# First mixer of a two-mixer decoder step: values and decayed keys turned by VectorE and a DRAM scratch instead of by TensorE

## The reference

```python
def hgrn_layer(x, s0, norm_g, w_in, g_norm, w_o, lb):
    proj = rms_norm(x, norm_g) @ w_in
    q, fz, i, gate = jnp.split(proj, [hk, 2 * hk, 2 * hk + A_WIDTH], axis=-1)
    q = silu(q)
    logf = jnp.logaddexp(jnp.log(lb), jnp.log1p(-lb) + log_sigmoid(fz))
    k = (1.0 - lb) * sigmoid(-fz)
    v = i
    o, s_t = gated_recurrence(q, k, v, logf, s0, chunk)
    o = rms_norm(o, g_norm) * silu(gate)
    return x + o @ w_o, s_t
...
def step(s, inp):                      # one chunk of one head
    cum = jnp.cumsum(gc, axis=2)
    o_inter = einsum('bhtk,bhkv->bhtv', qc * exp(cum), s)
    decay = exp(where(causal, cum[:, :, :, None, :] - cum[:, :, None, :, :], -inf))
    att = einsum('bhtk,bhsk,bhtsk->bhts', qc, kc, decay)
    o = o_inter + einsum('bhts,bhsv->bhtv', att, vc)
    s_new = exp(last)[..., None] * s + einsum('bhsk,bhsv->bhkv', kc * exp(last - cum), vc)
```

## Time and profile before

| | |
|---|---|
| Median of 3 runs | 1513.93 us (1513.2 to 1513.94) |
| The profiled execution's own time | 1510.86 us |
| Its span, first to last instruction | 1509.1 us |
| TensorE busy | 1476.7 us, 98% |
| VectorE busy | 987.5 us, 65% |
| ScalarE busy | 677.9 us, 45% |
| GpSimd busy | 418.0 us, 28% |
| Mixer A's heads | from 51.58 us to some 592.8 us of the span |
| One inner head (head 3) | 68.15 us |

### The profile page before, as it was taken

How to read it: one execution, slowest core, us unless ns; L and a number is a source line. 1 busy time by engine, 2 the same in 40 slices (tenths; PEclk the granted TensorE clock), 3 DMA queues, 4 the chain that set the end, 5 groups by cost and what they waited for, 6 DMA issues and landing times.

```text
span 1509.1 us, 23379 instructions
## 1 busy us (share of the span) xinstructions
PE 1476.7 (98%) x8437; PEld 1089.3 (72%) x8437; DVE 987.5 (65%) x1987; ACT 677.9 (45%) x1380; POOL 418.0 (28%) x335
## 2 busy tenths in 40 slices
PE   6999999999999999999999999999999999998998
PEld 6788888888888885445777777777777777763443
DVE  5878696878778694126467676868777676757321
ACT  4444555444444453212265555645555555545100
POOL 5012322121212201012051535354352625422200
PEclk9999999999999999999999999999999999999999
DMA  9683939476583933423236859696877869598731
GB/s 275 186 234 103 292 95 267 137 208 184 164 228 113 291 140 111 126 64 129 62 112 191 271 180 310 191 278 201 270 247 229 274 214 308 179 341 329 242 131 58
DMA packets 290505, 300.53 MB, mean 199 GB/s; under 512 B 25863, under 2 KB 247295, under 8 KB 290391
## 3 DMA queue, kind: packets, MB, share of 16 engines
q1 hardware_dynamic: 279254, 262.44, 57.1%
q0 software_dynamic: 11136, 36.59, 6.7%
HBM read 243.57 MB, written 122.53 MB: 243 GB/s over the span
## 4 chain that ended last, share of the span: by engine, by line
PE 86%; DVE 5%; ACT 4%; DMA 2%; issue 2%; SPq 0%; POOL 0%; DVEq 0%; POOLq 0%
PE psum L2145 44%; PE psum L2169 7%; PE psum L2659 7%; PE psum L2457 5%; PE psum L2483 4%; PE psum L2222 3%; PE psum L2108 2%; PE psum L2417 2%; PE psum L2515 2%; ACT psum L1281 1%; PE psum L2308 1%; PE psum L2292 1%; PE psum L2233 1%; ACT psum L1290 1%; PE psum L2310 1%
## 5 line engine op out<-in xcount | busy, mean ns | idle before, releaser
L2145 PE MATMUL psum<-arena 128*128 128x252 f32 (+1 forms) x3472 | 811.9, 385 | 2.3 <-DVE arena L1458 2.2
L2145 PEld LDWEIGHTS psum<-arena 128*128 128x128 f32 x3472 | 640.7, 190 | 124.8 <-issue 23.1
L956 POOL TENSOR_TENSOR arena<-arena 128x1024 f32<-128x1024 f32 x64 | 156.8, 2450 | 377.8 <-DMA arena<-k_pages 373.1
L1458 DVE TENSOR_TENSOR arena<-arena,psum 128x252 f32<-128x252 f32 (+1 forms) x310 | 128.9, 416 | 160.0 <-PE psum L2145 155.1
L2659 PE MATMUL psum<-arena 128*128 128x512 f32 x256 | 113.9, 597 | 1.6 <-DVE arena L1872 1.6
L2169 PE MATMUL psum<-arena 128*128 128x512 f32 x256 | 113.0, 594 | 0.1
L1031 ACT COPY arena<-psum 128x252 f32<-128x252 f32 (+1 forms) x124 | 46.2, 372 | 138.3 <-PE psum L2145 138.2
L2659 PEld LDWEIGHTS psum<-arena 128*128 128x128 f32 x256 | 47.1, 190 | 59.4 <-issue 57.0
L2169 PEld LDWEIGHTS psum<-arena 128*128 128x128 f32 x256 | 47.5, 190 | 57.4 <-issue 56.5
L1094 ACT ACTIVATE arena<-arena 128x1024 f32<-128x1024 f32 x48 | 50.7, 1056 | 84.6 <-DVE arena L1504 84.2
L1281 ACT ACTIVATE psum<-psum,arena 128x640 f32<-128x640 f32 (+3 forms) x64 | 58.9, 921 | 61.0 <-DVE arena L1805 61.0
(11 more groups left out here) (272 smaller groups left out, 2083.2 us busy)
## 6 DMA issues: line engine op xcount, KB each, us to landing
k_pages<-in_cache_k SPq DMA_DIRECT2D x64, 512.0 KB, 6.5
v_pages<-in_cache_v SPq DMA_DIRECT2D x64, 512.0 KB, 7.1
arena<-k_pages SPq DMA_DIRECT2D x64, 512.0 KB, 5.4
arena<-v_pages SPq DMA_DIRECT2D x64, 512.0 KB, 6.8
arena<-in_w_in_a SPq DMA_DIRECT2D x32, 512.0 KB, 6.8
arena<-in_x_prompt SPq DMA_DIRECT2D x16, 512.0 KB, 7.5
arena<-in_w_kv SPq DMA_DIRECT2D x16, 512.0 KB, 6.8
arena<-in_w_in_b SPq DMA_DIRECT2D x16, 512.0 KB, 8.0
```

The costliest lines, as they stand in the source:

```text
L956: pool.tensor_tensor(k_ring[:, m % 2], k_ring[:, m % 2], q_all[:, m % S:m % S + 1, :].broadcast_to([P, PAGES, P]), ALU.mult).then_inc(kq_m ...
L1458: dve.tensor_tensor(out, more, bank[n % 2][:, 0:size(u)], ALU.add).then_inc(of.by_dve, 1)
L2145: ins = pe.matmul(bank[n % 2][:, 0:size(u)], w[:, k, :], x[:, k, :], start=(k == 0 and r in (0, 1, 3, 4)), stop=(k == HK - 1), skip_group_ ...
```

## The change

In mixer A the sixteen transposes of a head on TensorE (L2258 and L2276) and ScalarE's four copies (L1121, L1146) are gone. VectorE turns V and the decayed keys in blocks of 32 x 32 from SBUF to SBUF (`turn_tokens`); SP writes each to a DRAM tensor `token_rows` with four DMAs and reads it back with one (`tokens_out`, `tokens_in`), which puts the blocks in place. After the way back the 128 columns of a chunk stand in four groups of 32 that are apart from one another, so where V or the keys are the stationary operand, each matmul becomes four of 32 columns: 32 instead of 8 for the state updates, and 32 instead of 8 for V by att. The updates move behind `fq(9)` (in the last head behind `fq(8)`), and the state part of the outputs into a loop of its own. The exponential for `k_dec` and `k_dec` itself move ahead, and `k_dec` lies in `t1` now. The copy of `o_row` moves ahead of the gate's step. SP's sorting of pages is cut in two halves of 8 DMAs a head. On GpSimd the F and Q sums of head h + 2 are made at the end of `head(h)`, from unit 11 of the running `fq` on, and the store of `s_smp` goes ahead of the V and G sums.

```diff
@@ VectorE
+                def turn_tokens(n, out, src):
+                    dve.transpose(out.rearrange("p (r t l) -> p t r l", r=4, l=32),
+                                  src.rearrange("p (t r l) -> p t r l", r=4, l=32)).then_inc(blocks_turned, 2)
...
                 factors(2)
                 fq(1)
+                dve.wait_ge(*units.taken(vg_unit(h, 9)))
+                dve.wait_ge(*units.taken(vg_unit(h, 12)))
+                turn_tokens(0, v_blocks, raw_v[:, 0:T])
                 merge(4)
+                a("exp_kd")
+                dve.tensor_tensor(k_dec, k_h[:, 0:T], t1[:, 0:T], ALU.mult).then_inc(vecs.sem, 1)
+                dve.wait_ge(vecs.sem, vecs.at("k_dec", h))
+                turn_tokens(1, k_blocks, k_dec)
                 a("s_kept")
...
                 merge(2)
                 fq(4)
-                a("exp_kd")
-                dve.tensor_tensor(k_dec, k_h[:, 0:T], t1[:, 0:T], ALU.mult).then_inc(vecs.sem, 1)
                 merge(1)
                 fq(5)
+                dve.wait_ge(smp_done.sem, smp_done.at("o_row", h))
+                dve.tensor_copy(o_row, bank[6][:, 0:2 * P]).then_inc(vecs.sem, 1)
                 a("ln_g")
...
-                dve.wait_ge(smp_done.sem, smp_done.at("o_row", h))
-                dve.tensor_copy(o_row, bank[6][:, 0:2 * P]).then_inc(vecs.sem, 1)
...
+                fq(8)
                 chunk_states(0)
-                fq(8)
                 chunk_states(1)
@@ SP
-            for h in range(AH - 1):
-                sp.wait_ge(units.done, vg_unit(h, 14))
...
-                sort_pages(sp, h + 1)
...
+            for s, half in ((0, 0), (0, 1), (1, 0)):
+                sort_pages(sp, s, half)
+            def tokens_out(h, n, blocks):
+                sp.wait_ge(blocks_turned, 2 * token_set(h, n))
+                if h:
+                    sp.wait_ge(pt_moved, MOVES * token_set(h - 1, n))
+                dst = token_rows[n].rearrange("(r l) (g n) -> g l r n", r=4, g=4)
+                for g in range(4):
+                    src = blocks[32 * g:32 * g + 32].rearrange("p (r n) -> p r n", r=4)
+                    sp.dma_start(dst[g], src).then_inc(rows_stored, 16)
+            def tokens_in(h, n, blocks):
+                sp.wait_ge(rows_stored, STORES * token_set(h, TOKEN_SETS - 1 if h == AH - 1 else n))
+                sp.dma_start(blocks, token_rows[n]).then_inc(pt_moved, 16)
+            for h in range(AH):
...
+                if h < AH - 1:
+                    tokens_out(h, 0, v_blocks)
+                sp.wait_ge(units.done, vg_unit(h, 14))
+                if h + 2 < AH:
+                    load_w(sp, h // 2 + 1, h % 2)
+                elif h + 2 == AH:
+                    sp.dma_start(w_o[:, 0:AH // 2], w_o_rows[:, 0:AH // 2]).then_inc(w_o_loaded, 16)
+                else:
...
+                    tokens_out(h, 0, v_blocks)
+                if h < AH - 1:
+                    tokens_in(h, 0, v_blocks)
+                    tokens_out(h, 1, k_blocks)
+                else:
+                    tokens_out(h, 1, k_blocks)
+                    tokens_in(h, 0, v_blocks)
+                tokens_in(h, 1, k_blocks)
+                if h < AH - 1:
+                    sort_pages(sp, h + 1, 1)
...
+                    if h + 2 < AH:
+                        sort_pages(sp, h + 2, 0)
@@ TensorE
-                    for t in range(4 * j, 4 * j + 4):
-                        ins = pe.transpose(bank[4 + j][:, t % 4 * P:(t % 4 + 1) * P], raw_v[:, cols(t)], ident)
...
-                    for t in range(4 * j, 4 * j + 4):
-                        ins = pe.transpose(bank[4 + j][:, t % 4 * P:(t % 4 + 1) * P], k_dec[:, cols(t)], ident)
...
-                fq(8, 9, 10)
+                fq(8)
+                if h + 1 < AH:
+                    fq(9)
+                pe.wait_ge(pt_moved, MOVES * token_set(h, 1))
+                for j in range(2):
+                    pe.wait_ge(uu_taken_v, 4 * h + 5 + j)
+                    for c in range(4 * j, 4 * j + 4):
+                        for g in range(4):
+                            ins = pe.matmul(bank[4 + j][32 * g:32 * g + 32, c % 4 * P:(c % 4 + 1) * P], k_dec_tok[:, block_of(c), g],
+                                            v_tok[:, block_of(c)], start=True, stop=True, skip_group_check=True)
+                    ins.then_inc(uu_done.sem, 1)
+                if h + 1 == AH:
+                    fq(9)
+                fq(10)
...
+                    for g in range(4):
+                        pe.matmul(bank[6 + t // 4][32 * g:32 * g + 32, t % 4 * P:(t % 4 + 1) * P], v_tok[:, t, g], att[:, cols(t)],
+                                  start=(t % 4 == 0), stop=(order[t] == 0), skip_group_check=True)
@@ GpSimd, head(h)
-                if h + 1 < AH:
-                    if h:
-                        pool.wait_ge(units.done, fq_unit(h, 14))
-                    w_sums(h + 1, F, Q, sums_fq, fq_sums)
+                if h == 0:
+                    w_sums(1, F, Q, sums_fq, fq_sums)
                 if 0 < h < AH - 1:
                     o_store(h - 1)
+                pool.wait_ge(uu_taken_v, 4 * h + 6)
+                pool.dma_start(state_out[h], s_smp).then_inc(state_stored, 16)
                 if h + 1 < AH:
                     pool.wait_ge(units.done, vg_unit(h, 14))
                     w_sums(h + 1, V, G, sums_vg, vg_sums)
-                pool.wait_ge(uu_taken_v, 4 * h + 6)
-                pool.dma_start(state_out[h], s_smp).then_inc(state_stored, 16)
                 pool.wait_ge(uu_taken_v, 4 * h + 8)
                 pool.dma_start(prompt_out[h], s_all[:, NC - 1, :]).then_inc(prompt_stored, 16)
+                if h + 2 < AH:
+                    pool.wait_ge(units.done, fq_unit(h + 1, 11))
+                    w_sums(h + 2, F, Q, sums_fq, fq_sums, last_free=(units.done, fq_unit(h + 1, 13)))
```

More of the change, by code:

```diff
@@ L487, in build, with token_set @@
         HEAD = (slice(0, DH), slice(DH, P))
+        def token_set(h, n):
+            return TOKEN_SETS * h + n + 1
         def row_banks(i):
@@ L545, in page_id, with sort_pages @@
             return sp.value_load(at, min_val=0, max_val=n_pool - 1)
-        def sort_pages(sp, s):
-            for j in range(PAGES):
+        def sort_pages(sp, s, half):
+            for j in range(HALF * half, HALF * half + HALF):
                 page = page_id(sp, s * PAGES + j)
@@ L585, in _ @@
-            sp.wait_ge(o_stored, 16 * (AH - 2))
-            sp.wait_ge(vecs.sem, vecs.at("q", AH - 1))
-            for h in range(EARLY):
-                sp.dma_start(o_heads[h], o_dram[h]).then_inc(early_loaded, 16)
-            sp.wait_ge(units.done, vg_unit(AH - 1, 14))
-            for h in range(EARLY, AH - 2):
-                sp.dma_start(o_heads[h], o_dram[h]).then_inc(o_loaded, 16)
-            sp.dma_start(w_o[:, AH // 2:AH], w_o_rows[:, AH // 2:AH]).then_inc(w_o_loaded, 16)
-            LF_STEP = -(-S * PAGES // (TT - 1))
+            for s, half in ((0, 0), (0, 1), (1, 0)):
+                sort_pages(sp, s, half)
@@ L816, in _, with block_sums @@
             me = Steps(pool, w_steps)
-            def block_sums(one, two, out, done):
+            def block_sums(one, two, out, done, last_free=None):
                 me.did(pool.tensor_tensor(out[:, 0], two[:, 0:HK], two[:, HK:KT], ALU.add))
@@ L1116, in head @@
                 level(8)
+                for t in range(NC):
+                    end = t * P if t >= NC // 2 else t * P + C - 1
+                    ins = act.activation(t1[:, cols(t)], cum[:, cols(t)], ACT.Exp, bias=cum[:, end:end + 1], scale=-1.0)
+                ins.then_inc(acts.sem, 1)
                 level(4)
                 level(2)
-                for j in range(2):
-                    act.wait_ge(uu_done.sem, uu_done.at(f"v_turn{j}", h))
-                    act.copy(v_tok[:, 4 * j:4 * j + 4, :], bank[4 + j][:, :]).then_inc(uu_taken_a, 1)
                 fq(0)
@@ L1133, in head @@
                 fq(2)
-                for t in range(NC):
-                    end = t * P if t >= NC // 2 else t * P + C - 1
-                    ins = act.activation(t1[:, cols(t)], cum[:, cols(t)], ACT.Exp, bias=cum[:, end:end + 1], scale=-1.0)
-                ins.then_inc(acts.sem, 1)
                 act.wait_ge(*units.taken(vg_unit(h, 13)))
@@ L1143, in head @@
                 act.activation(sg_h, sg_h, ACT.Ln, bias=1.0).then_inc(acts.sem, 1)
-                for j in range(2):
-                    act.wait_ge(uu_done.sem, uu_done.at(f"turn{j}", h))
-                    act.copy(k_dec_tok[:, 4 * j:4 * j + 4, :], bank[4 + j][:, :]).then_inc(uu_taken_a, 1)
                 v("o_smp")
@@ L2271, in head @@
                 fq(5)
-                v("k_dec")
-                for j in range(2):
-                    pe.wait_ge(uu_taken_v, 4 * h + 5 + j)
-                    for t in range(4 * j, 4 * j + 4):
-                        ins = pe.transpose(bank[4 + j][:, t % 4 * P:(t % 4 + 1) * P], k_dec[:, cols(t)], ident)
-                    ins.then_inc(uu_done.sem, 1)
```

(14 more changed lines are left out.)

70 lines of the change are left out of this document (36 added, 34 removed).

## The result

The changed kernel takes **1538.64 us** (median of four runs, 1537.44 to 1541.54); the kernel before, run beside it, 1513.58 us. The ratio is 1.0165 [1.0153, 1.0177]: slower, by 25.1 us. The prediction was slower by 9.2 us, 1523 with a range up to 1532; the sign is right, the size is not, and the time lies above the range.

A forecast was written before the change was run, and what follows sets the result against it. TensorE, busy for 98% of the span, was taken as the bound. Six heads +6.9, head 6 -0.45, head 7 +2.8 gave +9.2 us on the 1513.93 median: 1523, range 1506 to 1532.

The forecast's parts named there:

- What leaves and what comes on TensorE: TensorE, each head: transposes leave (-1.76 us), strips come (+0.56), net -1.20 us without a new wait.
- The strips' part: State updates and V by att in 32-column strips on TensorE: +0.28 us a block, +0.56 a head.
- Rival D: TensorE's strips stop overlapping in runs of 64: 7.1 us a block, +85 us, 1599; chance 0.01.
- VectorE's turns: Two block transposes a head, 0.6 to 1.25 us each; V turned by 292.4, K by 295.6, hidden from TensorE.
- K's wait: TensorE before state updates, for K's DRAM round trip: 2.5 us a head taken, 2.8 worked out.
- rival C: K's blocks return from DRAM before TensorE asks, transfers at 405 GB/s: -8.5 us, 1505.4; chance 0.24.
- The sums made sooner: GpSimd's F and Q sums a head sooner: TensorE waits for none of them, priced at zero.
- rival E: VectorE late for fact1 or merges, transposes slowed beside GpSimd: 1 to 2 us a head, 1522; chance 0.03.
- Head 7: Last head: V by att starts +2.5 us later behind K's and V's reloads, +0.28 for strips: +2.8 us.
- A: The wait before the state updates decides, as summed: 1523, own range 1517 to 1532; chance 0.58.
- B: The wait just eats the saving: 0.6 to 1.6 us in each of seven heads, about 1514; chance 0.14.
- F: GpSimd's sums made sooner do nothing: 0 us, held true in all cases, no separate chance.

The follow-up runs named there:

- late_w: Changed kernel with the next weights' load (or first half of w_o) issued behind K's reload instead of ahead of V's: 1506.27 us, ratio 0.9957.
- strips: Kernel before with only the state updates and V by att in 32-column strips, transposes kept: 1518.57 us, ratio 1.003.
- w_first: Changed kernel with SP issuing the next weights (w_o in head 6) ahead of V's stores: 1518.64 us, ratio 1.0035.
- upd_late: Changed kernel with state updates two units later, behind fq(11), and VectorE's gate step ahead of chunk_states; DMAs untouched: 1508.72 us, ratio 0.9969.
- sums_later: Changed kernel with GpSimd's F and Q sums waiting for unit 12 instead of 11, nothing else: 1533.94 us, ratio 1.0133.
- sums_only: Kernel before with only GpSimd's F and Q sums made a head sooner: 1512.89 us, ratio 0.9996.
- late_w_split: late_w with the waits for q_dec and chunk_states moved behind the last units' V-by-att strips: 1505.91 us, ratio 0.9953.
- sums_back: Changed kernel with GpSimd's F and Q sums of head h + 1 back at their old place, at the start of head h: 1535.26 us, ratio 1.0144.
- best2: late_w_split with GpSimd's F and Q sums starting one unit later: 1504.45 us, ratio 0.9935.
- w_first_sums: w_first with GpSimd's F and Q sums back at their old place: 1514.33 us, ratio 1.0002.

## Why the prediction was right and wrong

**What leaves and what comes on TensorE: right.** -1.20 us a head was forecast without a new wait; `late_w`, whose inner heads have no wait, gives 67.04 against 68.15, -1.11. The strips' part was 0.56, `strips` measured 0.65 a head: the updates 1.88 to 1.89 us as said with the way in, the output block a little dearer. Rival D had no case.

**VectorE's turns: right, at the dear end.** The block transpose from SBUF takes 1.24 us; V is turned at 302.97, which is 292.4 on the old scale (10.53 us later in the span), the number given. K is turned at 306.09, 295.6 on the old scale, again the number given.

**K's wait: the mechanism right, the size 2.5 against some 3.0 in heads 1 to 5.** On the old scale TensorE reaches the updates at 309.7 (forecast 309.6) and K's tokens are there at 312.9; the working had found 312.4, a wait of 2.8, and I then took 2.5 of it. K out was issued at 300.8, not 299, because V's way back took 1.81 us to issue behind the weights (0.34 where none are just ahead), and it landed at 309.5 against 308.4; the way back then took 3.3 us where 3.6 were put. That the wait is the queue's doing, and not the turn's, is shown twice: it goes when the weights are behind K (`late_w`) and when they are ahead of V's stores (`w_first`). `upd_late` shows only that TensorE's own work can cover it. Heads 0 to 6 waited 18.2 us in all where 15.9 were summed (six of 2.5 and one of 0.9). I had written that the forecast was wrong if K out ended within 6 us of its first issue: it took 8.76, so rival C, all at 405 GB/s, was not near in this order of the queue. The Trainium skill ("DMA: Bandwidth & Descriptors", Anatomy of one DMA) prices a DMA that GpSimd issues at 2 us and bytes over 436 GB/s, an estimate of 3.2 us for this half megabyte. SP issues these stores, and the nearest case, V's in `late_w`, took 3.76 us; K's, always beside others, took 5.4 us and more wherever SP issued them.

**The sums made sooner, priced at zero: this step failed.** It said that "TensorE waits for none of the sums today, so zero; their cover is the second half of a head". True of who waits for the sums, and the wrong question. What counts is what the sums lie beside. At the new place they start 0.51 us into the gate step (in head 0 at its start), which reads two tensors in SBUF, and it takes 4.11 us for 1.29 (3.56 in head 0); the add behind it is late and TensorE stands 1.52 us in five heads and 0.88 in one, 8.5 in all and 0.2 of restart each: +9.7 us. The prediction named such a collision for the V and G sums in its own rows (1.40 against 0.68) and gave it to rival E, "VectorE becomes late", at 0.03, with another place in view. `sums_later` shows the cause, as it moves nothing but the sums, and `w_first` that it doesn't need K's wait; `sums_only` shows that the same edit is free in the kernel before, where the sums start 0.4 us ahead of the gate step and it takes 1.96. The Trainium skill ("GPSIMD Engine Reference", Specifications) says that GpSimd shares its SBUF interfaces with VectorE and that they contend where VectorE's instruction has two SBUF inputs. These traces agree: 4.11 us for 1.29. They add that the price is several-fold, and that the distance of the starts alone doesn't fix who pays: at 0.52 us into the step it took 4.12 in one run (`late_w_split`, head 0) and 1.29 in another (`late_w`, head 0). What decides it stays open.

**The clock: a term that was missing.** A wait was priced at its own length. In heads 0 and 7 the strips behind one also ran at the lower level, 1.55 and 1.4 us more. It is also why the second wait taken away alone gave so little: removing it (`sums_back`, `sums_later`) should have won 9.7 us, and by the medians 5 to 6 of them didn't come, 3.7 and 4.5 of which the rows of the strips show, as five heads' updates now ran at the lower clock; with K's wait gone as well (`late_w`, `best2`) the updates take 1.95 us in all eight heads. Why the updates of the changed kernel's heads 1 to 5 stay at 1.95 us behind waits just as long isn't settled. They do in every one of these heads while the second wait stands there, but head 4 of `sums_back` does too, behind 3.02 us and without that wait.

**Head 7: right in sum, by other parts.** +2.8 forecast, +3.65 measured: only 0.76 us for K (3.1 worked out), then 2.43 for `chunk_states` and the clock.

**The rivals.** Of A the wait for K came true and the time did not: it lies above A's own range of 1517 to 1532. B (the wait eats the saving) and C did not come true. F (the sums do nothing) is true alone in the kernel before and false in the changed one.

**The sum.** Forecast +9.2. To it come +9.7 for the second wait, +2.3 for the longer waits for K in heads 0 to 6, +1.55 for head 0's block at the lower clock, +0.85 in head 7 and +0.6 for the strips: 24.2, against 25.1 between the medians. (The spans differ by 28.0; 3.07 of that is how far the profiled execution of before lies under its median.)

## What to carry to other kernels

Work moved on an engine that nobody waits for is not free until it is known what it will run beside: look up each instruction of VectorE with two SBUF inputs near the new place of a GpSimd operation, and keep the two apart; a start of one inside the other went either way here. A round trip through DRAM should be queued ahead of every large load that isn't due yet; here moving one load in SP's program turned +25 us into -7, part of it because the second wait went too. And waits on the bounding engine don't add up: of one taken away about half can be lost again to the clock, so take them away together and measure.

## What was not expected of the hardware

- VectorE's gate step (128x1032) takes 1.29 us alone, 1.96 where GpSimd's sums started 0.4 us ahead of it, and 4.11 in most heads where they start 0.51 or 0.52 us behind its start. The step that makes `logf`, of the same size, takes 1.23 alone, 1.36 where the sums had started 2.24 us ahead, 1.98 at 1.63 us (head 1 of the kernel before), and 3.08 at 0.52 us.
- Either engine can be the slowed one: with the sums 0.4 us ahead GpSimd's second took 2.26 us instead of 1.28, and in heads 0 and 2 of `late_w`, with the sums 0.52 us behind the start of the gate step, the step took 1.29 and 1.28 and GpSimd's first sum 1.89 and 1.90. (The profile's times on GpSimd are rough.)
- Scans of 128x512 take 1.20 to 1.22 us alone and 2.18 to 2.22 beside GpSimd's third and fourth sum.
- Four stores of 128 KB in 1 KB pieces take 3.76 us from first issue to landing with nothing else in SP's queue (V's in `late_w`), 6.8 with a reload ahead and GpSimd's 512 KB store beside (K's in `late_w`), and 8.76 behind the weights (K's in the changed kernel, all head 3).
- Behind waits of 2.4 to 3.6 us the block of 64 strips took 2.7 to 3.6 us in some heads instead of 1.95 (granted clock 0.52 to 0.55 in the blocks of 3.35 to 3.6 us that were looked at, 0.71 in the one of 2.67), and 1.95 behind waits of the same length in others. The last head's wait of 2.43 us for `chunk_states` has the same length in every kernel that has it, and the block behind it took 1.95 us in `sums_back`, 2.67 in `late_w` and 3.61 in `w_first_sums`.
